# Retention scans that read the accumulation banks, and value weights centred in two halves

## The reference, cut to what matters

```
def retention_chunked(q, k, v, log_gamma, s0):
    scores = jnp.einsum('bnihd,bnjhd->bnhij', qc, kc) * dec
    o_intra = jnp.einsum('bnhij,bnjhe->bnihe', scores, vc)
    w_k = jnp.exp(log_gamma[:, None] * (RET_CHUNK - 1 - pos)[None, :])
    kv = jnp.einsum('bnjhd,hj,bnjhe->bnhde', kc, w_k, vc)
    chunk_decay = jnp.exp(log_gamma * RET_CHUNK)[:, None, None]
    def step(s, kv_n):
        return chunk_decay * s + kv_n, s
    _, s_prev = lax.scan(step, s0, jnp.moveaxis(kv, 1, 0))
    w_q = jnp.exp(log_gamma[:, None] * (pos + 1.0)[None, :])
    o_cross = jnp.einsum('bnihd,hi,nbhde->bnihe', qc, w_q, s_prev)
    return o_intra + o_cross
# run forward and backward (own decays, start states from the context), summed,
# then per head: (o - mean(o)) * rsqrt(var(o) + EPS) * g, times silu(gate)
```

## Time and profile before

| | |
|---|---|
| median of 3 runs (2749.69 to 2751.81) | 2749.9 us |
| the profiled execution's own time | 2746.85 us |
| its span | 2745.0 us |
| TensorE busy, share of the span | 96% |
| VectorE, ScalarE, GpSimd busy | 53%, 39%, 17% |
| mean granted TensorE clock | 0.988 |
| inb's last tile and the way into rv | 253 to 274 us of the span |
| retention | 338 to 405 us of the span |

### The profile page before, as it was taken

How to read it: one execution, slowest core, us unless ns; L and a number is a source line. 1 busy time by engine, 2 the same in 40 slices (tenths; PEclk the granted TensorE clock), 3 DMA queues, 4 the chain that set the end, 5 groups by cost and what they waited for, 6 DMA issues and landing times. The chain is left out here.

```text
span 2745.0 us, 36345 instructions
## 1 busy us (share of the span) xinstructions
PE 2630.6 (96%) x14641; PEld 2282.5 (83%) x14641; DVE 1460.4 (53%) x2041; ACT 1060.6 (39%) x1788; POOL 480.2 (17%) x321
## 2 busy tenths in 40 slices
PE   6999979999999999999999999999999999999999
PEld 2777767899777888888888999878989998878977
DVE  5745483333457666666657624447743624426751
ACT  3411534443335343343345224247731223237740
POOL 0001211242100000000000001038820002009930
PEclk9999989999999999999999999999999999999999
DMA  5542101000211121121121315232122213233222
GB/s 238 174 140 101 55 5 54 16 1 1 100 47 42 51 62 47 47 62 47 46 62 41 109 43 124 59 93 56 44 95 92 66 49 86 59 108 83 48 85 84
DMA packets 69683, 193.68 MB, mean 71 GB/s; under 512 B 8080, under 2 KB 26896, under 8 KB 68624
## 3 DMA queue, kind: packets, MB, share of 16 engines
q1 hardware_dynamic: 69520, 191.41, 23.0%
HBM read 148.88 MB, written 19.07 MB: 61 GB/s over the span
## 5 line engine op out<-in xcount | busy, mean ns | idle before, releaser
L2677 DVE SCALAR_TENSOR_TENSOR res<-ps,gates,res 128x1024 f32<-128x1024 f32 x120 | 148.6, 1279 | 100.0 <-PE ps L2802 100.0
L1315 PE MATMUL ps<-h_hi,pf_wh 128*128 128x346 f32 (+2 forms) x800 | 184.5, 334 | 0.2
L2536 ACT ACTIVATE wo_wh<-ff_raw 128x512 fp32r<-128x512 f32 x120 | 75.3, 628 | 278.7 <-DVE ff_raw L2647 114.2
L1315 PE MATMUL ps<-h_lo,pf_wh 128*128 128x346 f32 (+2 forms) x800 | 183.0, 333 | 0.0
L1946 DVE TENSOR_REDUCE da_negmax<-ps 128x1 f32<-128x1040 f32 x136 | 167.5, 1236 | 18.8 <-PE ps L1796 11.6
L1931 POOL TENSOR_TENSOR da_E<-da_E,da_F 128x1040 f32<-128x1040 f32 x68 | 164.6, 2421 | 5.7
L2802 PE MATMUL ps<-ff_h_hi,wo_wh 128*128 128x512 f32 x512 | 157.8, 389 | 1.4 <-DVE res L2677 1.3
L1839 PE MATMUL ps<-da_aT,v 128*128 128x128 f32 (+1 forms) x1224 | 157.5, 274 | 0.7 <-ACT qk L1903 0.7
L2802 PE MATMUL ps<-ff_h_hi,wo_wl 128*128 128x512 f32 x512 | 157.6, 389 | 0.0
L2802 PE MATMUL ps<-ff_h_lo,wo_wh 128*128 128x512 f32 x512 | 157.6, 389 | 0.0
L905 POOL MEMSET h_hi<- 128x112 f32 x2 | 0.4, 194 | 870.8 <-POOLq L66 870.8
(11 more groups left out here) (546 smaller groups left out, 6227.2 us busy)
## 6 DMA issues: line engine op xcount, KB each, us to landing
ff_raw<-w_ff SPq DMA_DIRECT2D x48, 512.0 KB, 3.5
ada_w<-w_ada SPq DMA_DIRECT2D x16, 1024.0 KB, 7.4
ff_raw<-w_in SPq DMA_DIRECT2D x20, 512.0 KB, 4.1
pf_raw<-w_in SPq DMA_DIRECT2D x20, 512.0 KB, 4.0
wo_raw<-w_out SPq DMA_DIRECT2D x18, 512.0 KB, 4.6
residual_spill<-res SPq DMA_DIRECT2D x16, 520.0 KB, 3.1
st_q<-st_q_rounded SPq DMA_DIRECT2D x32, 260.0 KB, 5.2
ada_w<-w_ada SPq DMA_DIRECT2D x4, 2048.0 KB, 17.0
```

The lines of the kernel that those rows point to most:

```text
L1315: pe.matmul(bank(i * 2 + s, s)[c], wh[:, s, q * P:(q + 1) * P], x(q)[:, a:a + ln], start=(q == 0 and n == 0), stop=False)
L2536: act.activation(ring(wh, i), src, ACT.Copy).then_inc(s_hi, 1)
L2677: last = dve.scalar_tensor_tensor(out=res[:, m, :], in0=k.ps[:, b:b + 2, :].rearrange("p c w -> p (c w)"), scalar=gate[:, m:m + 1], in1=re ...
```

## The change

1. `centre` takes a range of tiles and is called at m = 3 for tiles 0 to 3 and at m = 4 for tiles 4 to 7. SP issues the load of the first half behind the fourth modulation sum and of the second behind the fifth. Each store has a semaphore of its own; the fetch for the next phase waits for the first store alone, and a new `sp_last` waits for the second at the end of the phase.
2. Scans 0 to 4 read their newest increment from the bank (`fresh`) where they read ACT's copy before; scan 0 keeps one input from the copy. PE waits before it writes a bank again until the scan that reads it has run. The copies by ACT stay.
3. GpSimd zeroes first and then decays the queries of all four heads; DVE's two decays are gone. The first scores wait for the four zeroings, the first outputs for all twelve GpSimd instructions.

```diff
+    def centre(self, dve, tiles_):
+        for q in tiles_:
             if q % 4 == 0:
                 dve.wait_ge(self.s_w[q // 4], 16)
...
-        sp.wait_ge(self.ada.s_sum, 5)
         for x, rows in enumerate(halves(self.w)):
+            sp.wait_ge(self.ada.s_sum, 4 + x)
             sp.dma_start(self.raw[:, 4 * x:4 * x + 4, :], rows).then_inc(self.s_w[x], 16)
         for x, rows in enumerate(halves(self.w_centred)):
             sp.wait_ge(self.s_centred, 4 * x + 4)
-            sp.dma_start(rows, self.raw[:, 4 * x:4 * x + 4, :]).then_inc(self.s_stored, 16)
-        sp.wait_ge(self.s_stored, 32)
+            sp.dma_start(rows, self.raw[:, 4 * x:4 * x + 4, :]).then_inc(self.s_stored[x], 16)
+        sp.wait_ge(self.s_stored[0], 16)
+
+    def sp_last(self, sp):
+        sp.wait_ge(self.s_stored[1], 16)
...
-        if m == 4:
-            self.centre(dve)
+        if m >= 3:
+            self.centre(dve, range(4 * m - 12, 4 * m - 8))
...
                     if i == 0:
                         pe.wait_ge(s_kz, RH)
-                        pe.wait_ge(s_p, 8)
+                        pe.wait_ge(s_p, 4)
...
                     if i == 0:
-                        pe.wait_ge(s_p, 10)
-                        pe.wait_ge(s_qs, 2)
+                        pe.wait_ge(s_p, 12)
...
                     if m >= 4:
                         pe.wait_ge(s_out, m - 3)
+                        pe.wait_ge(s_f, (m - 4) // 2 + 1)
...
                 c = Chain(pool, s_p)
-                for h in range(2):
+                for h in range(RH):
+                    c(pool.memset(kz[other(h), h, :], 0.0))
+                for h in range(RH):
                     for r in range(2):
                         c(decayed(pool, h, r))
-                for h in range(RH):
-                    c(pool.memset(kz[other(h), h, :], 0.0))
-                for r in range(2):
-                    c(decayed(pool, 2, r))
...
-                steps = [((fw, S[fw, 0, :], kv[fw, NCK, :], kv[fw, NCK + 1, :]),
-                          (bw, S[bw, NCK - 1, :], kv[bw, NCK + 1, :], kv[bw, NCK, :]))]
+                fresh = lambda part, n: k.ps[part, 2 + order.index(n) % 4, :]
+                steps = [((fw, S[fw, 0, :], fresh(fw, NCK), kv[fw, NCK + 1, :]),
+                          (bw, S[bw, NCK - 1, :], fresh(bw, NCK + 1), kv[bw, NCK, :]))]
...
-                    steps.append(((fw, S[fw, n + 1, :], S[fw, n, :], kv[fw, n, :]),
-                                  (bw, S[bw, m - 1, :], S[bw, m, :], kv[bw, m, :])))
+                    add = fresh if n < NCK // 2 else (lambda part, n: kv[part, n, :])
+                    steps.append(((fw, S[fw, n + 1, :], S[fw, n, :], add(fw, n)),
+                                  (bw, S[bw, m - 1, :], S[bw, m, :], add(bw, m))))
...
-                for r in range(2):
-                    decayed(dve, RH - 1, r).then_inc(s_qs, 1)
```

More of the change, by code:

```diff
@@ L452, in open @@
         self.s_w = [self.k.sem(f"centre_w{i}") for i in range(2)]
-        self.s_total, self.s_centred, self.s_stored = (self.k.sem(f"centre_{n}") for n in ("total", "done", "stored"))
-    def centre(self, dve):
-        for q in range(KD):
+        self.s_total, self.s_centred = (self.k.sem(f"centre_{n}") for n in ("total", "done"))
+        self.s_stored = [self.k.sem(f"centre_stored{i}") for i in range(2)]
+    def centre(self, dve, tiles_):
+        for q in tiles_:
             if q % 4 == 0:
@@ L1514, in retention @@
         s_t, s_kw, s_kv, s_out, s_f, s_p = (k.sem(f"retk_{n}") for n in ("turned", "kw", "kv", "out", "scanned", "pool"))
-        s_kz, s_qs = (k.sem(f"retk_{n}") for n in ("keys", "queries"))
+        s_kz = k.sem("retk_keys")
         s_s, s_d, s_o, s_sq, s_sd, s_r, s_z, s_tr, s_po = (k.sem(f"reto_{n}") for n in (
```

## The result

The changed kernel takes **2731.8 us** (median of 4 runs, 2730.2 to 2733.0) against 2750.9 us of the kernel before on the same chip (4 runs, 2749.7 to 2753.0). The ratio is 0.993, with a 95% interval of 0.992 to 0.994.

A forecast was written before the change was run, and what follows sets the result against it. TensorE was busy 2630.6 of 2745.0 us, so only its waits could be won: 1.8 at the values plus 9.4 at retention's head, 11.2, giving 2735.7 profiled and, with 3.05 added, 2738.7 us; range 2734.5 to 2743.

The forecast's parts named there:

- Part 1: Way from inb into the values: centring in halves lets ScalarE evacuate tile 5 sooner; values start 1.8 us earlier.
- Part 2: Head of retention: bank-reading scans and decays moved off VectorE bring the first outputs earlier, saving 9.4 us (7.4 to 10.0).
- 361.3 as a floor: Head of retention: GpSimd's zeroings and eight decays let the first outputs start no earlier than 361.3.
- the 0.6 put on top of it: Head of retention: first outputs taken at 361.9, between 361.3 and 363.9, to allow for TensorE's lower clock level.
- Rival 2: Head of retention: TensorE at its lower clock is the chain, outputs at 363.9, time 2740.7 us; chance 0.17.
- Bank operands: Scans 0 to 4: reading one operand from a bank was taken to cost 0, against the skill's estimated 2.6 us.
- the added waits on TensorE: Head of retention: TensorE's waits for a scan before rewriting its bank never come last, cost 0.
- rival 4: Head of retention: GpSimd holds the scans whatever their inputs, outputs 5.5 us later, time 2753.6 us; chance 0.04.
- sum of terms on VectorE's chain: Head of retention: scan 0 saves 3.08, scan 1 4.15, the two decays 2.47; sum 9.7, outputs at 361.6.
- all but meet: Head of retention: GpSimd's 361.3 and VectorE's 361.6 were said to nearly coincide in setting the first outputs.
- rival 1: Start of the values: TensorE's clock stays up across the barrier, 2.9 us more saved, time 2735.8 us; chance 0.15.
- the median of the runs shown stands 3.05 above it: Whole kernel: 3.05 us between profiled execution and median, added to 2735.7 to give 2738.7 us.

The follow-up runs named there:

- retention alone: The kernel before with both retention edits (scans reading banks, GpSimd zeroing first and decaying all queries) and the old centring: 2736.4 us against 2751.2.
- more filler: The kernel before with 52 filler matmuls behind inb in place of 16, ahead of the barrier before the values: 2748.5 us against 2749.7.
- the full shift: The changed kernel with 71 more filler matmuls ahead of the latent keys, the phase after retention: 2743.7 us against 2749.1 of the kernel before.
- GpSimd decays alone: The kernel before with GpSimd zeroing first and decaying all queries, scans still reading SBUF: 2748.4 us against 2751.2.
- centring alone: The kernel before with only the centring in halves, retention as before: 2744.3 us against 2751.2.

## Why the prediction was wrong, and where it was right

**Part 1, 1.8 us:** 1.9, by the mechanism foretold. ScalarE's evacuation follows TensorE's last matmul, and the store at 255.9 holds nobody.

**Part 2, 9.4 us:** 9.7. Scans 0 to 4 run at 2.3 us beside decays of 2.42; GpSimd's chain (23.4 us from its start) sets the first outputs. The prediction's 361.3 as a floor held to 0.3 us, and the 0.6 put on top of it for TensorE's lower level wasn't needed: its increments ran at 1.06 and 1.16 us once the idle times had shrunk to 1.2 to 1.6. Rival 2 fell by that. Bank operands cost nothing, the added waits on TensorE cost nothing, rival 4 is what the GpSimd half alone does and the bank reads prevent.

That the measured 9.7 equals the prediction's sum of terms on VectorE's chain is luck. That chain became 12.4 us shorter: the decayed scores came 32.6 us after retention's start (370.55 − 337.93) and now come 20.2 after it (353.45 − 333.27). Beyond the terms of the sum, 1.6 are scan 0 starting at +4.5 in place of +6.1, since TensorE ran at its full level, and 1.1 the wait for the last chunk's keys, which is gone. In retention alone, with scan 0 at +6.1, the scores came at +21.8, and the outputs at +23.64 all the same. So VectorE and GpSimd did not "all but meet": GpSimd alone sets the outputs, which start 3.5 us after VectorE's decayed scores (0.75 before), and the saving is what its chain leaves, 33.37 − 23.69.

**The first step that failed: rival 1, given 0.15.** The clock does stay up across the barrier, and the values are 2.75 us shorter. The prediction argued that a level which holds for 6 us of busy time would fall after 1.6 us of idle time as well. That was an argument from how long the low level lasts to what brings it about. The trace of before had rows on the latter which the prediction didn't use, the other barriers. One is

```profile
2126.37 1.80 PE L1085 MATMUL ps<-ident,ones 128*128 128x128 f32 x14 [1.74 <-PEq L66]
```

Fourteen fillers in 1.80 us are 0.13 each, the full level, after 1.74 us of idle time. At 405.45, shown above, 28 of them take 6.05 us, 0.22 each: most of them ran at the low level after 1.56 us. There TensorE had been idle for 1.62 more shortly before; but that isn't the whole reason, since in the trace of more filler the same two idle times were followed by 28 fillers in 3.36 us, the full level. Of the eleven other barriers in the trace of before, with 0.91 to 1.74 us of idle time, two were followed by the low level within 2 us (those at 59.3 and 405.5). The rows thus spoke for the rival, and its chance should have been at least even. That the clock at this barrier can be held by filling the idle time alone is shown by the experiment with more filler.

**The second step that failed: "the median of the runs shown stands 3.05 above it".** The prediction carried the distance between the profiled execution of before and its median over to the changed kernel as a constant. It isn't one, nor a property of a kernel. In the runs beside the result it was 4.0 for before, and −1.15 for the changed kernel; with the second profile of each it was −6.6 (2747.4 − 2753.98) and 1.4 (2731.05 − 2729.65). The sum: forecast for the profiled execution 2735.7, measured 2732.97, a miss of 2.7, which is rival 1; forecast for what lies on top of it +3.05, measured −1.15, a miss of 4.2. Together 6.9, the distance from 2738.7 to 2731.8. With the first miss alone the time would have been 2736.0, with the second alone 2734.5, on the range's lower edge. It took both to put it outside.

What the second step is made of is shown in part. Executions of before differ by when the granted clock falls in later stages, one of which cost 4.2 us in a trace, and filler there takes about that off the median. That stage keeps its clock behind the attention in every trace of the changed kernel. *Why* it does is not shown and stays open. It isn't the shift in time (the full shift didn't undo it), nor the length of the idle time ahead of it (1.48 us in executions of either kind). By the medians all kernels in which the retention half or a part of it was changed gained some 5 to 7 us more than they did in place, even GpSimd decays alone, which made retention longer; centring alone gained 2 more (by the ratio nothing), filler alone nothing. That is a pattern over medians of 5 to 12 runs, and no mechanism.

## What to carry to other kernels

Before moving elementwise work to GpSimd, look at what VectorE does meanwhile: with two SBUF operands it stood still here for as long as each GpSimd instruction read SBUF, and one operand left in the accumulation bank freed it at no price (2.29 us for eight either way). When a change shortens an idle time of TensorE at a barrier, look at each other barrier's idle time and clock in the same trace before deciding whether the low level will stay, and count them: the same idle time went both ways here. A forecast of a median from one profiled execution needs the spread of that kernel's executions as a term of its own: here it was 13 us wide, and 5 of the 19 us of measured gain were not between the two profiled executions. A second profile of each kernel would have shown it.

## What the hardware did that was not expected

- A VectorE instruction with two SBUF operands is held for a whole GpSimd instruction, not slowed by a share: 18.94 us for eight that need 2.29, beside eight decays of 2.41.
- At one barrier TensorE's clock held at 1.00 after 1.4 to 1.6 us of idle time in nine of nine executions; at another, 1.48 us were followed by a granted clock of 0.51 and 0.52 over 10 us in two executions (centring alone, more filler) and by the full level in ten. Idle time alone doesn't say what the clock will do.
- The values' loss isn't certain either: 3.25 us of idle time cost nothing in one execution, 3.39 to 3.80 cost 2.5 to 2.7 us in five.
